# Weaving the first dense group into the transposition of the input rows, with all low halves of x on VectorE and the masks built behind them

## What is computed

```python
h = layer_norm(h, ln_in_w, ln_in_b)
proj = u @ w_in
cb, cc, cx, q, k, v, g, a1, ga, gb = jnp.split(proj, idx, axis=-1)
gk = jax.nn.log_sigmoid((a1 @ w_a2 + b_a2).astype(jnp.float32)) / GATE_NORM
```

## Time and profile before

| | us |
|---|---|
| median of 3 runs (lowest to highest) | 1980.44 (1977.44 to 1980.49) |
| the profiled execution | 1981.62 |
| its span, first to last instruction | 1979.9 |
| TensorE busy in the span | 1925.6 (97%) |
| VectorE, ScalarE, GpSimd busy | 1087.9, 823.2, 360.5 |

### The profile page before, as it was taken

How to read it: one execution, slowest core, us unless ns; L and a number is a source line. 1 busy time by engine, 2 the same in 40 slices (tenths; PEclk the granted TensorE clock), 3 DMA queues, 4 the chain that set the end, 5 groups by cost and what they waited for, 6 DMA issues and landing times. The chain is left out here.

```text
span 1979.9 us, 35731 instructions
## 1 busy us (share of the span) xinstructions
PE 1925.6 (97%) x14197; PEld 1861.8 (94%) x14197; DVE 1087.9 (55%) x1158; ACT 823.2 (42%) x1048; POOL 360.5 (18%) x419
## 2 busy tenths in 40 slices
PE   6999999999999999999999899999999999999994
PEld 5999889998899988999899899999999999999994
DVE  5556555565555655556565675444544454445445
ACT  5534445434454343544443353333333333333331
POOL 4241212312032130321200141000100010001002
PEclk9999999999999999999999899999999999999997
DMA  5645675557654576545744555555555555555541
GB/s 177 188 142 156 211 214 153 148 145 231 199 156 144 143 240 193 160 139 146 236 163 158 149 150 168 164 165 168 162 168 163 166 165 166 167 159 169 170 155 53
DMA packets 176039, 330.12 MB, mean 167 GB/s; under 512 B 10964, under 2 KB 29584, under 8 KB 175672
## 3 DMA queue, kind: packets, MB, share of 16 engines
q1 hardware_dynamic: 161016, 291.21, 49.3%
q0 software_dynamic: 4960, 18.42, 2.9%
q10 hardware_dynamic: 9968, 19.16, 2.8%
HBM read 307.36 MB, written 21.38 MB: 166 GB/s over the span
## 5 line engine op out<-in xcount | busy, mean ns | idle before, releaser
L346 DVE TENSOR_TENSOR w_lo<-raw,w_hi 128x1024 fp32r<-128x1024 f32 x544 | 723.3, 1333 | 803.0 <-ACT w_hi L341 802.9
L341 ACT ACTIVATE w_hi<-raw 128x1024 fp32r<-128x1024 f32 x544 | 574.7, 1058 | 915.0 <-PE bank L368 903.1
L366 PE MATMUL bank<-x_hi,w_hi 128*128 128x288 f32 (+2 forms) x3072 | 916.7, 298 | 4.5 <-DVE x_lo L392 2.9
L367 PE MATMUL bank<-x_lo,w_hi 128*128 128x288 f32 (+2 forms) x3072 | 911.1, 297 | 0.0
L368 PE MATMUL bank<-x_hi,w_lo 128*128 128x288 f32 (+2 forms) x3072 | 908.7, 296 | 0.0
L366 PEld LDWEIGHTS bank<-x_hi,w_hi 128*128 128x128 f32 x3072 | 578.5, 188 | 14.8 <-issue 10.4
L367 PEld LDWEIGHTS bank<-x_lo,w_hi 128*128 128x128 f32 x3072 | 578.6, 188 | 4.1 <-issue 2.9
L368 PEld LDWEIGHTS bank<-x_hi,w_lo 128*128 128x128 f32 x3072 | 577.8, 188 | 0.0
L368 PE MATMUL bank<-f_hi,w_lo 128*128 128x288 f32 x1280 | 379.5, 296 | 0.0
L366 PE MATMUL bank<-f_hi,w_hi 128*128 128x288 f32 x1280 | 378.9, 296 | 0.0
L367 PE MATMUL bank<-f_lo,w_hi 128*128 128x288 f32 x1280 | 373.2, 292 | 0.0
(11 more groups left out here) (227 smaller groups left out, 1048.7 us busy)
## 6 DMA issues: line engine op xcount, KB each, us to landing
raw<-in_w SPq DMA_DIRECT2D x256, 512.0 KB, 3.7
raw<-in_w_in SPq DMA_DIRECT2D x224, 512.0 KB, 3.7
out<-S ACTq DMA_DIRECT2D x36, 512.0 KB, 4.8
raw<-in_w_in SPq DMA_DIRECT2D x64, 256.0 KB, 3.0
S<-in_state_gla POOLq DMA_DIRECT2D x32, 512.0 KB, 6.9
raw<-in_w_o SPq DMA_DIRECT2D x32, 512.0 KB, 3.6
out<-yrow SPq DMA_DIRECT2D x8, 192.0 KB, 2.2
xrow<-in_x_prompt SPq DMA_DIRECT2D x2, 512.0 KB, 7.7
```

Of the source, the lines that this page charges most:

```text
L341: nc.scalar.activation(w_hi[:, s, :, :], raw[:, s, :, :], ACT.Copy).then_inc(hi_ready, 1)
L346: nc.vector.tensor_tensor(w_lo[:, s, :, :], raw[:, s, :, :], w_hi[:, s, :, :].bitcast(F32), ALU.subtract).then_inc(lo_ready, 1)
L366: nc.tensor.matmul(out, wh, a_hi[:, kt, c0:c1], start=(kt == 0), stop=False)
L367: nc.tensor.matmul(out, wh, a_lo[:, kt, c0:c1], start=False, stop=False)
```

## The change

- The rows are normalised in halves of 1024 columns, each block of rows with its own semaphore `rows_ready`: ScalarE takes both halves of block 0 and the second of block 1, VectorE both of block 2 and the first of block 1. Blocks 0 to 7 of x need the first halves alone.
- TensorE transposes six blocks (`X_LEAD`), then begins group 0. Behind each of its units 0 to 4 come two more blocks, and behind units 1 to 6 the gate pairs that `GATE_AFTER` lists. A unit also waits for the low halves of its own two blocks.
- ScalarE works unit by unit: two `hf`, then the `w_hi` of that unit (that of unit 0 ahead of all `hf`). VectorE: two times `x_hi` and `x_lo`, then `w_lo`.
- VectorE makes all 16 `x_lo`; GpSimd waits for the last of them before it starts the masks.
- SP loads `wa1` behind the first two units of group 0, where it was ahead of them.

The core of the diff; the parts left out rename semaphores, drop the old loops and skip group 0 in the later loops of splits:

```diff
+X_LEAD = 6
+GATE_AFTER = {1: range(0, 4), 2: range(4, 6), 3: range(6, 8), 4: range(8, 10), 5: range(10, 12), 6: range(12, KT)}
...
+            def start_step(unit):
+
+                for k in (UK * unit + X_LEAD, UK * unit + X_LEAD + 1):
+                    if k < KT:
+                        x_transposed(k)
+                for k in GATE_AFTER.get(unit, ()):
+                    gate_rank(k)
+
+            for k in range(X_LEAD):
+                x_transposed(k)
...
-                    dense_group(pe, HG * h + j, x_hi, x_lo, GROUP_COLS[j], after=sequences(h, j))
+                    if h == 0 and j == 0:
+                        dense_group(pe, 0, x_hi, x_lo, GROUP_COLS[0], after=start_step,
+                                    operand=lambda i: (x_lo_ready, UK * (i + 1)))
+                    else:
+                        dense_group(pe, HG * h + j, x_hi, x_lo, GROUP_COLS[j], after=sequences(h, j))
...
+            act.wait_ge(row_scale, 1)
+            normalise_half(0, 0)
+            normalise_half(0, 1)
             act.wait_ge(g_full[0], 1)
             nc.scalar.activation(params[:, :], gbank[0][:, 0:P_ALL], ACT.Copy).then_inc(g_free[0], 1)
-            normalise_rows(2, T - 2 * P, 2)
+            split_hi(act, 0, 0)
...
+            for i in range(UNITS):
+                for k in (UK * i, UK * i + 1):
+                    n = k % X_BANKS
+                    act.wait_ge(g_full[n], X_FIRST[n] + k // X_BANKS + 1)
+                    if k >= HF_SLOTS:
+                        act.wait_ge(x_lo_ready, k - HF_SLOTS + 1)
+                    nc.scalar.activation(hf[:, k % HF_SLOTS, :], gbank[n][:, 0:T], ACT.Identity,
...
+                if i == 0:
+                    act.wait_ge(row_scale, 2)
+                    act.wait_ge(rows_ready[1], 1)
+                    normalise_half(1, 1)
+                else:
+                    split_hi(act, 0, i)
+                if i == 2:
+                    act.wait_ge(wa1_landed, 16)
+                    act.wait_ge(const_ready, 1)
+                    nc.scalar.activation(wa1_parts[:, :, 0:RANK], wa1[:, :, 0:RANK], ACT.Copy).then_inc(wa1_split, 1)
...
+            dve.wait_ge(row_pow, 2)
+            normalise_half(2, T - 2 * P, 0)
             dve.wait_ge(row_pow, 3)
+            normalise_half(1, P, 0)
+            normalise_half(2, T - 2 * P, 1)
+            for i in range(UNITS):
+                for k in (UK * i, UK * i + 1):
+                    n = k % X_BANKS
+                    dve.wait_ge(g_free[n], X_FIRST[n] + k // X_BANKS + 1)
+                    nc.vector.tensor_copy(x_hi[:, k, :], hf[:, k % HF_SLOTS, :]).then_inc(x_hi_ready, 1)
                     dve.wait_ge(x_hi_ready, k + 1)
                     nc.vector.tensor_tensor(x_lo[:, k, :], hf[:, k % HF_SLOTS, :], x_hi[:, k, :].bitcast(F32),
-                                            ALU.subtract).then_inc(x_lo_ready[0], 1)
+                                            ALU.subtract).then_inc(x_lo_ready, 1)
+                split_lo(dve, 0, i)
...
-            for k in range(1, KT, 2):
-                pool.wait_ge(x_hi_ready, k + 1)
-                nc.gpsimd.tensor_tensor(x_lo[:, k, :], hf[:, k % HF_SLOTS, :], x_hi[:, k, :].bitcast(F32), ALU.subtract)\
-                    .then_inc(x_lo_ready[1], 1)
+            pool.wait_ge(x_lo_ready, KT)
             seq(nc.gpsimd.memset(mask[:, :, :], 0.0))
```

More of the change, by code:

```diff
@@ L215, in build @@
         x_hi_ready = sem("x_hi_ready")
-        x_lo_ready = [sem("x_lo_ready_even"), sem("x_lo_ready_odd")]
+        x_lo_ready = sem("x_lo_ready")
         wa1_split = sem("wa1_split")
         a1_low_ready = sem("a1_low_ready")
+        rows_ready = [sem(f"rows_ready{i}") for i in range(3)]
         pool_seq = sem("pool_seq")
@@ L445, in _ @@
                     if first is not None:
-                        load_group(HG * h + j, w_in, 0, first + h * GW)
+                        load_group(HG * h + j, w_in, 0, first + h * GW, load_wa1 if h == 0 and j == 0 else None)
                         continue
@@ L492, in _ @@
             last.then_inc(g_full[1], 1)
[L495 to L518, removed]
@@ L519, in _, with x_transposed @@
-            last.then_inc(g_full[3], 1)
+            def x_transposed(k):
+                n = k % X_BANKS
+                if X_FIRST[n] + k // X_BANKS > 0:
+                    pe.wait_ge(g_free[n], X_FIRST[n] + k // X_BANKS)
+                for i, rows in enumerate([P, P, T - 2 * P]):
+                    if k == 0:
+                        pe.wait_ge(rows_ready[i], 1)
+                    if k == KT // 2:
+                        pe.wait_ge(rows_ready[i], 2)
+                    last = transpose(gbank[n][:, i * P:i * P + rows], xrow[0:rows, i, k * P:(k + 1) * P], rows)
+                last.then_inc(g_full[n], 1)
@@ new lines, in gate_rank @@
+            def gate_rank(kt):
+                if kt == 0:
+                    pe.wait_ge(wa1_split, 2)
+                pe.wait_ge(x_lo_ready, kt + 1)
+                high = (gbank[3][0:RANK, 0:T], wa1_parts[:, kt, 0:RANK], x_lo[:, kt, :])
+                both = (gbank[3][0:WA_W, 0:T], wa1_parts[:, kt, :], x_hi[:, kt, :])
+                if kt == 0:
+                    nc.tensor.matmul(*both, start=True, stop=False)
+                    nc.tensor.matmul(*high, start=False, stop=False)
+                else:
+                    nc.tensor.matmul(*high, start=False, stop=False)
+                    last = nc.tensor.matmul(*both, start=False, stop=(kt == KT - 1))
+                    if kt == KT - 1:
+                        last.then_inc(g_full[3], 1)
@@ L739, in _, with normalise_half @@
                                  accum_out=sums[0:T - 2 * P, 1:2]).then_inc(sums_ready, 1)
[L741 to L747, removed]
+            def normalise_half(i, q):
+                c = slice(q * (D // 2), (q + 1) * (D // 2))
+                nc.scalar.activation(xrow[:, i, c], xrow[:, i, c], ACT.Identity, bias=nbias[:, i:i + 1],
+                                     scale=rstd[:, i:i + 1]).then_inc(rows_ready[i], 1)
@@ L754, in _ @@
-            act.wait_ge(const_ready, 1)
-            nc.scalar.activation(wa1_parts[:, :, 0:RANK], wa1[:, :, 0:RANK], ACT.Copy).then_inc(wa1_split, 1)
             act.wait_ge(g_free[0], 1)
[L757 to L766, removed]
@@ L767, in _ @@
-            for i in range(2, SLOTS):
-                split_hi(act, 0, i)
+            for i in range(UNITS):
[5 more added lines that the diff above has]
+                    nc.scalar.activation(hf[:, k % HF_SLOTS, :], gbank[n][:, 0:T], ACT.Identity,
+                                         bias=params[:, P_INB + k:P_INB + k + 1],
+                                         scale=params[:, P_INW + k:P_INW + k + 1]).then_inc(g_free[n], 1)
+                if i == 0:
+                    act.wait_ge(row_scale, 2)
+                    act.wait_ge(rows_ready[1], 1)
+                    normalise_half(1, 1)
+                else:
+                    split_hi(act, 0, i)
[3 more added lines that the diff above has]
+                    nc.scalar.activation(wa1_parts[:, :, 0:RANK], wa1[:, :, 0:RANK], ACT.Copy).then_inc(wa1_split, 1)
@@ L827, in head @@
                     g = HG * h + j
-                    for i in range(SLOTS, UNITS):
+                    for i in range(UNITS if g == 0 else SLOTS, UNITS):
                         split_hi(act, g, i, with_k=(h if j == 1 else None))
@@ L1488, in _ @@
                     .then_inc(row_pow, 1)
-                if i != 1:
+                if i != 2:
                     pool.wait_ge(row_pow, m + 1)
```

27 lines of the change are left out of this document (12 added, 15 removed).

## The result

| | before | after |
|---|---|---|
| median of five runs, us (lowest to highest) | 1978.70 (1977.44 to 1980.49) | 1987.24 (1985.82 to 1988.71) |
| the profiled execution | 1981.62 | 1986.22 |
| its span | 1979.9 | 1984.5 |

What follows compares the result with a forecast made beforehand. TensorE, busy 97% of the span, was taken as the bound. Products 1.3 us later plus 2.7 at half clock, on 1981.62, gave 1985.6; half of that execution's 1.2 above the median was set off: 1985.0 us, range 1980 to 1989.

Steps and rivals of the forecast that it cites:

- Start of the group: TensorE's first dense matmul, after six transposed blocks of x: at 21.9 us instead of 38.41.
- the clock's rise: TensorE's clock in the first dense group: rises from half to full at 27 us, ends 25 and 34.
- Rival 3: Clock rises only in the woven group's second unit, at about 33: 2.6 us later, 1987.6 us; chance 0.16.
- End of the group: TensorE's first dense group ends at 59.3 us, 4.7 us before the 64.0 of the kernel before.
- Last low half: VectorE's sixteenth x_lo, which GpSimd's masks wait for: done at 49.3 us.
- Masks to issue: GpSimd from first mask memset to the issue of wa2h's load: 13.3 us, between 11.05 and 14.77.
- Landing: The load of wa2h from issue to landing: 2.7 us, so it lands at 65.3.
- Start of the products: TensorE's products with wa2h: start at 65.4, 1.3 us later than before, between -0.9 and +2.8.
- Half clock behind the wait: After TensorE's idle wait for wa2h the clock falls to half: 2.7 us lost, ends 0 and 4.
- A shift of TensorE near the start reaches the end one for one: Behind the first matmul, TensorE busy 97% with few gaps: an early shift changes the total time equally.
- Rival 1: On GpSimd, wa2h's load lands before the woven group ends, so the kernel is faster: 1976.3 us; chance 0.07.

Runs made afterwards that it cites:

- idle products: Changed kernel plus 62 matrix products nobody reads, on TensorE ahead of its wait for wa2h: 1987.14 us (1.0034), run once more 1987.35 us (1.0034).
- the later comparison: The changed kernel run once more, unaltered, on one chip beside its version with 62 unread products: 1987.19 us, 1.0031 of the kernel before.
- the first attempt at late masks: Kernel before, unwoven, with waits for x_lo_ready[0] and the first four w_lo put ahead of the masks; both met by 38 us: 1980.58 us (0.9998).

## Why the prediction was right, step by step

The kernel became slower, as forecast, and its time lies in the range, 2.2 us above the forecast of 1985.0. The mechanism is the one that it named: the masks' delay passes to the load, the load to TensorE. That the number came so close is in part luck: two errors, 3.7 us too little before the products' start and 3.45 us that came back behind it, nearly cancel. Its terms, in order:

- *Start of the group*: 21.9 forecast, 21.99 measured; the clock's rise at 27 and 27.2. Rival 3 (a late rise) did not come. The rise is read from the pace, 0.24 apart up to 26.98 and 0.13 from 27.41 on; the windows print 1.00 for the start of both profiles, so the lower level stands there by this pace alone, which the earlier trace rows have at 0.50.
- *End of the group*: 59.3 forecast, 60.2 measured. ScalarE and VectorE did not bound it: TensorE's list has no wait between 22 and 60 us.
- *Last low half*: 49.3 forecast; it ended at 50.0.
- *Masks to issue*: 13.3 forecast, 14.19 measured, inside the bounds. The stretched operations were others than assumed. Out of VectorE's way the selects on `mask` took 2.24 and 2.26 us; the six on `segmask` took 4.88 beside four `w_lo`.
- *Landing*: **this term was mis-sized.** I took the shortest of four landings, 2.7; it was 4.8. The step failed in not asking what else the DMA engines would carry at 64 us. The raw units of group 1 are issued by SyncE as each `w_lo` frees a slot, and those four ended at 63.9, just ahead of the load. With them held back it lands in 2.2.
- *Start of the products*: +1.3 forecast, +5.0 measured: 0.7 from the last low half, 0.9 from the masks, 2.1 from the landing.
- *Half clock behind the wait*: 2.7 forecast, 2.77 measured on the spot. But the idle products took it away, and the total stayed. As a term of the total it is not confirmed in full.
- *"A shift of TensorE near the start reaches the end one for one"*: **this step failed ahead of the layer norm.** 3.45 of 7.75 us came back there, 2.1 of it in waits that the kernel before had further on. It hid the mis-sized landing: forecast +4.0 on the profiled execution, +4.6 measured. Behind the layer norm the sentence holds: in all fourteen profiled runs the time less the start of the restart there is 851.2 to 851.6 us. What varies lies between the products' start and that restart, 1064.2 to 1068.6 us: at half clock behind the wait 1065.6 to 1068.6 (four profiles, mean 1067.2), at the full clock 1064.2 to 1068.6 (ten, mean 1065.8). So of the 2.77 us about half shows there on average, within a wide spread.

By all runs the loss is larger than by the two profiles: the ratio 1.0038 is 7.5 us, 1.0031 in the later comparison 6.1, where 4.6 were forecast (1985.0 against 1980.44). The profiled execution after lies 1.0 under its median, that before above its own. Rival 1, the load landing before the group ends, was priced at 1976.3; the kernel that does it measured 1976.27. The products' start carries most of the total: in all fourteen profiled runs the time less that start is 1915.8 to 1919.9 us, while the start itself goes from 59.2 to 69.3.

## What to carry to other kernels

A small load at the end of an engine's queue inherits every delay of the work ahead of it. Before you delay set-up work, look at what stands behind it, and put the load where its buffer comes free: three places did that here, and each turned a loss of 6 to 8 us into a gain of 4 to 5. Price a load by how long the DMA engines will still be busy at the time at which it will be issued, not by what it took elsewhere. And measure a gain of the clock in the total: on the spot it was 2.77 us here, in the total of the runs with idle products none was seen.

## What the runs showed of the hardware that was not expected

- The same 16 KB load took 2.0 to 2.2 us to land where the DMA share over its way was 0.03 to 0.21, and 4.6 to 5.0 at 1.02 to 1.07. The share at the issue does not tell it alone: in the kernel before with its masks behind the seventh `w_lo` the load was issued at a share of 0.99 and landed in 2.0 us. There the share had fallen to 0.08 by 64.0, 1.5 us behind the issue; in the changed kernel it stayed at 1.02 all the way.
- GpSimd and VectorE slowed each other in both directions, and VectorE's operations unequally: beside the selects its casts took 397 ns instead of 315 and the row normalisation (48x1024, mean of two) 1156 instead of 798, the subtractions with two inputs 485 instead of 476. The Trainium skill, "GPSIMD Engine Reference", 1. Specifications, names both kinds, those with two SBUF inputs and those in a 2-port mode; the prediction had drawn on the first alone, and here the one-input operations lost far more. In which mode they ran no row shows.
- With the same work on TensorE up to then, the clock rose at 34.1 us in the profiled execution of the kernel before, at 32.9 in that of the first attempt at late masks and at 27.4 in that with the masks behind the seventh `w_lo`; in the first and the last of these the group ended at 64.0 and at 61.8. In the woven kernels it rose between 24.9 and 27.9. All these are read from the pace of the matmuls; what sets the time of the rise was not tried.
